# Moved turning products, two more split gate blocks, and a reordered router in a two-stage transformer kernel

## The reference, cut to what matters

```
proj = rmsnorm(x, g_mix) @ w_in          # q, k, v, index q/k, conv input, memory q, 3 x 1024 gate logits
o_a = top-k attention(rope(rmsnorm(q)), rope(rmsnorm(k)), v)      # 8 heads of 64, 2 key heads
o_b = silu(layernorm(causal depthwise conv(a * sigmoid(g), 31 taps)))
k_m, v_m = split(rmsnorm(mem, g_mem) @ w_mem_kv)                  # 256 memory tokens
o_m = memory attention(rmsnorm(q_m, g_qm), rmsnorm(k_m, g_km), v_m)
gates = sigmoid(gate_logits + b_gate)
x = x + (gates[0]*(o_a @ w_br_a) + gates[1]*(o_b @ w_br_b) + gates[2]*(o_m @ w_br_m)) @ w_o
h = rmsnorm(x, g_ffn)
router: best of 4 groups, then the 2 best of its 8 experts; out = sum of combine * (silu(a)*b) @ w_down
x = x + out
second block: silu(c) @ w_ada gives shifts, scales and gates of each layer (c has 1024 values)
```

## Time and profile before

| | us |
|---|---|
| median of 3 runs | 1892.06 |
| lowest and highest | 1891.32, 1894.72 |
| the profiled execution | 1889.99 |
| its span, first to last instruction | 1888.2 |
| TensorE busy | 1841.8 (98%) |
| VectorE busy | 1173.6 (62%) |
| ScalarE busy | 780.9 (41%) |
| mean DMA rate | 207 GB/s |

### The profile page before, as it was taken

The page is one execution under the profiler, slowest core; times in us unless marked ns, Lnnn a source line. Parts: engine busy times, 40 slices in busy tenths (PEclk is TensorE's granted clock), DMA queues, the critical chain, the costliest instruction groups (busy, mean ns, idle before and its releaser), DMA issues.

```text
span 1888.2 us, 29939 instructions
## 1 busy us (share of the span) xinstructions
PE 1841.8 (98%) x12476; PEld 1661.0 (88%) x12476; DVE 1173.6 (62%) x1777; ACT 780.9 (41%) x1081; POOL 0.2 (0%) x4
## 2 busy tenths in 40 slices
PE   9999999899999999999999999999999999989999
PEld 8879889788866668999988889999999997879999
DVE  3875456566666656877547458776876547545543
ACT  2325442534444445434443234344443444324432
POOL 0000000000000000000000000000000000000000
PEclk9999999899999999999999999999999999999999
DMA  8334311566899986876530057876686341043451
GB/s 316 132 130 158 137 68 35 239 233 241 321 395 370 376 320 236 342 302 260 199 134 23 23 204 287 331 301 258 256 320 253 157 157 45 6 152 133 181 201 68
DMA packets 65222, 391.59 MB, mean 207 GB/s; under 512 B 7360, under 2 KB 7488, under 8 KB 27328
## 3 DMA queue, kind: packets, MB, share of 16 engines
q1 hardware_dynamic: 64800, 389.61, 53.4%
q10 hardware_dynamic: 288, 0.08, 0.0%
HBM read 388.61 MB, written 1.05 MB: 206 GB/s over the span
## 4 chain that ended last, share of the span: by engine, by line
PE 88%; DVE 7%; ACT 2%; issue 1%; DMA 1%; DVEq 0%; SPq 0%; ACTq 0%
PE bank L510 87%; DVE region L2219 1%; PE bank L551 1%; ACT w_hi L1452 1%; DMA slab<-in_w_ffn_in 1%; DVE slab_low L1900 0%; DVE region L2182 0%; DMA slab<-in_w_up 0%; DVE region L1913 0%; DVE tiny L2181 0%; DVE region L2505 0%; DVE region L2482 0%; DVE region L2503 0%; DVE region L2173 0%; DVE region L2501 0%
## 5 line engine op out<-in xcount | busy, mean ns | idle before, releaser
L1900 DVE TENSOR_TENSOR slab_low<-slab,w_hi 128x2048 fp32r<-128x2048 f32 x152 | 348.2, 2292 | 201.8 <-ACT w_hi L1452 201.5
L510 PE MATMUL bank<-h_hi,w_hi 128*128 128x256 f32 x1408 | 391.6, 281 | 0.0
L510 PE MATMUL bank<-h_hi,slab_low 128*128 128x256 f32 x1408 | 390.9, 281 | 0.0
L510 PE MATMUL bank<-h_lo,w_hi 128*128 128x256 f32 x1408 | 380.2, 281 | 0.0
L1452 ACT ACTIVATE w_hi<-slab 128x2048 fp32r<-128x2048 f32 x152 | 291.0, 1916 | 151.1 <-DMA slab<-in_w_ffn_in 72.9
L510 PEld LDWEIGHTS bank<-h_hi,slab_low 128*128 128x128 f32 x1408 | 269.5, 191 | 0.0
L510 PEld LDWEIGHTS bank<-h_hi,w_hi 128*128 128x128 f32 x1408 | 264.7, 188 | 0.4
L510 PEld LDWEIGHTS bank<-h_lo,w_hi 128*128 128x128 f32 x1408 | 257.6, 188 | 0.0
L510 PE MATMUL bank<-gT_hi,d_hi 128*128 128x256 f32 x832 | 234.0, 281 | 0.8 <-DVE gT_lo L2097 0.8
L510 PE MATMUL bank<-gT_lo,d_hi 128*128 128x256 f32 x832 | 233.7, 281 | 0.0
L510 PE MATMUL bank<-gT_hi,d_low 128*128 128x256 f32 x832 | 233.6, 281 | 0.0
(11 more groups left out here) (279 smaller groups left out, 2826.0 us busy)
## 6 DMA issues: line engine op xcount, KB each, us to landing
slab<-in_w_ffn_in SPq DMA_DIRECT2D x88, 1024.0 KB, 8.6
slab<-in_w_up SPq DMA_DIRECT2D x64, 1024.0 KB, 8.8
region<-in_w_ada SPq DMA_DIRECT2D x112, 512.0 KB, 6.6
region<-in_w_ffn_out SPq DMA_DIRECT2D x44, 1024.0 KB, 4.8
region<-in_w_down SPq DMA_DIRECT2D x32, 1024.0 KB, 5.5
slab<-in_w_in SPq DMA_DIRECT2D x23, 1024.0 KB, 4.8
slab<-in_w_mix_in SPq DMA_DIRECT2D x20, 1024.0 KB, 7.9
hT<-in_w_ada SPq DMA_DIRECT2D x32, 512.0 KB, 5.7
```

The lines of the kernel that those rows point to most:

```text
L510: return nc.tensor.matmul(o, lhsT, rhs, start=start, stop=True, skip_group_check=True)
L1900: V_.tensor_tensor(slab_low[slot][:, :], slab[slot][:, :], w_hi[h % 3][:, :].bitcast(F), ALU.subtract)\
```

## The change

The three turning products are made behind all four blocks of memory queries, and the two duplicating products behind all four key blocks; ScalarE copies the duplicated key behind the four key copies accordingly. GATES_PLAIN is 2, so 22 gate blocks are split, there are 11 split slabs, and the convolution's sums are taken ahead of gate blocks 4 and 8. VectorE makes in_lo and the first slab's low part ahead of the four scalings of qm and km, the second slab's behind them. In the router ScalarE copies htok_lo directly behind htok_hi and signals tok_ready there, and makes the permutation copies ahead of the first weight slab's high part. Three warming products are left of the five ahead of the first unit. SyncE issues c behind the slabs of the second unit instead of ahead of all.

```diff
--- before.py
+++ after.py
@@ -162,7 +162,7 @@
 SHORT_FIRST, OUT_EARLY = 2, 4
 FFN_UNITS = 11
 GATHER_PLACES = 3
-GATES_PLAIN = 4
+GATES_PLAIN = 2
 VALUES = P + 8
 FIRST = P + 8
 SCORES_AT = {2: (0, 1), 3: (2, 3), 4: (4, 5), 5: (6, 7)}
@@ -848,7 +848,7 @@
             def moe():
                 members = [u for u in UNITS if u.seg == 0]
                 slabs_of(members[0])
-                keep_warm(5)
+                keep_warm(3)
                 for s in range(2):
                     ring_free(s)
                 for kc in range(KD // 2):
@@ -983,21 +983,17 @@
                     pair_sum(sq[:, 1:3, :])
                     pair_sum(sq[:, 3:5, :])
                     pair_sum(sq[:, 5, :])
-                if b == 15:
-                    pe.wait_ge(S["qka_normed"], w("qka_normed"))
-                    for x in range(2):
-                        pair_sum(B1["qa"][:, 2 * x:2 * x + 2, :], "rot", "dve")
-                    pair_sum(B1["ka"], "rot", "dve")
                 conv(b) if b < 8 else queries(b - 8) if b < 12 else memory(b - 12)
+            pe.wait_ge(S["qka_normed"], w("qka_normed"))
+            for x in range(2):
+                pair_sum(B1["qa"][:, 2 * x:2 * x + 2, :], "rot", "dve")
+            pair_sum(B1["ka"], "rot", "dve")
             for i in range(KD):
                 pe.wait_ge(S["memh"], w("memh"))
-            keys = projection(B1["memh"], 4, "act")
-            for b in range(4):
-                if b == 2:
-                    pe.wait_ge(S["ka_roped"], w("ka_roped"))
-                    for x in range(2):
-                        pair_sum(B1["ka"], f"dup{x}")
-                keys(b)
+            project(B1["memh"], 4, "act")
+            pe.wait_ge(S["ka_roped"], w("ka_roped"))
+            for x in range(2):
+                pair_sum(B1["ka"], f"dup{x}")
             vslab = [arrive().rearrange("p (k c) -> p k c", k=KD) for _ in range(2)]
             for t in range(NT):
                 ps = product("act")
@@ -1629,10 +1625,9 @@
                         rsqrt_of(take()[:, 0:n], rsB[:, 0:n], 1.0 / 64, C("small", 0, 1), "rs")
                 evac(B1["qm"][:, c, :])
             for c in range(4):
-                if c == 2:
-                    for x in range(2):
-                        evac(B1["kdup"][:, x, :])
                 evac(B1["km"][:, c, :])
+            for x in range(2):
+                evac(B1["kdup"][:, x, :])
             act.wait_ge(S["read_by_act"], w.n["read_by_act"])
             nc.scalar.activation(sq[:, 0:4, :], B1["qm"], ACT.Square)
             nc.scalar.activation(sq[:, 4:8, :], B1["km"], ACT.Square).then_inc(S["qkm_sq"], 1)
@@ -1701,20 +1696,20 @@
             for t in range(NT):
                 for x in range(2):
                     evac(htok_hi[:, t, x * 512:(x + 1) * 512], 512)
+            for t in range(NT):
+                for x in range(2):
+                    evac(htok_lo[:, t, x * 512:(x + 1) * 512], 512)
+            act.wait_ge(S["read_by_act"], w.n["read_by_act"])
+            act.sem_inc(S["tok_ready"], 1)
             act.wait_ge(S["router_top2"], w("router_top2"))
             for t in range(NT):
                 m = nc.scalar.activation(route("e21", t, 1), route("e8", t, 8)[:, 1:2], ACT.Exp,
                                          bias=route("nv1", t, 1))
             m.then_inc(S["router_exp"], 1)
-            up_high(0)
-            for t in range(NT):
-                for x in range(2):
-                    evac(htok_lo[:, t, x * 512:(x + 1) * 512], 512)
-            act.wait_ge(S["read_by_act"], w.n["read_by_act"])
-            act.sem_inc(S["tok_ready"], 1)
-            up_high(1)
             evac(permT[:, 0:2, :].rearrange("p i t -> p (i t)"), 512)
             evac(permT[:, 2, :])
+            up_high(0)
+            up_high(1)
             moe()
 
             for l in range(LAYERS):
@@ -2220,16 +2215,16 @@
                                                      ALU.mult, ALU.add))
             later()
             dve.sem_inc(S["conv_y"], 1)
+            dve.wait_ge(S["in_high"], w("in_high"))
+            dve.wait_ge(S["memh_used"], w("memh_used"))
+            V_.tensor_tensor(in_lo[:, :, :], hT[:, :, :], in_hi[:, :, :].bitcast(F), ALU.subtract)\
+                .then_inc(S["in_split"], 1)
+            gate_low(0)
             for x in range(4):
                 nm = "qm" if x < 2 else "km"
                 scale_rs(B1[nm][:, 2 * (x % 2):2 * (x % 2) + 2, :], col("g_qm" if x < 2 else "g_km"), 2)
             dve.sem_inc(S["qkm_normed"], 1)
-            dve.wait_ge(S["in_high"], w("in_high"))
-            dve.wait_ge(S["memh_used"], w("memh_used"))
-            V_.tensor_tensor(in_lo[:, :, :], hT[:, :, :], in_hi[:, :, :].bitcast(F), ALU.subtract)\
-                .then_inc(S["in_split"], 1)
-            for k in range(2):
-                gate_low(k)
+            gate_low(1)
             ps = take()
             for c in range(4):
                 ins = V_.scalar_tensor_tensor(B1["y"][:, c, :], ps[:, 0:T], -1.0 / 512, B1["y"][:, c, :],
@@ -2617,6 +2612,8 @@
                     sp.dma_start(d_raw[b], source(unit, "down")).then_inc(S[f"d_in{b}"], 16)
                 for n, unit in enumerate(members):
                     up_load(unit, source(unit, "up"))
+                    if n == 1 and unit.seg == 0:
+                        sp.dma_start(c_act, a["c_2"][0:1, :].broadcast_to([P, D])).then_inc(S["c_in"], 16)
                     if n == 1 and gate_sem:
                         sp.wait_ge(S[gate_sem], w(gate_sem))
                     if n:
@@ -2685,7 +2682,6 @@
                 m = a[part + ("_in_2" if which == "up" else "_out_2")]
                 row = (unit.group * FFN_UNITS + unit.x) * P
                 return m[row:row + P, :]
-            sp.dma_start(c_act, a["c_2"][0:1, :].broadcast_to([P, D])).then_inc(S["c_in"], 16)
             stream([u for u in UNITS if u.seg < 2], source)
 
             for l in range(LAYERS):
```

## The result

The change took the kernel from 1892.72 us (median of 4 runs, 1891.32 to 1894.72) to 1879.78 us (median of 4, 1878.06 to 1884.34): ratio 0.9935, 95% interval 0.9914 to 0.9955, a gain of 12.9 us (by the interval 8.5 to 16.3). The forecast was 1881.1. The profiled run of the changed kernel, 1884.34 us with a span of 1882.6, was the slowest of its four.

What follows compares the result with a forecast made beforehand. TensorE was taken as the bound, busy 1841.8 of 1888.2 us. The terms 3.45 + 1.06 + 6.45 = 10.96 us, off the median 1892.06, gave 1881.1; forecast 1880 to 1882.5 (0.60), whole range 1878.5 to 1885.5.

Steps and rivals of the forecast that it cites:

- Part 1: Turning products: a plain projection block fills the 3.88 us gap ending at 101.00, leaving 0.43 idle; 3.45 us saved.
- Parts 2 and 3: Gate blocks: two more split blocks save 1.06 us; the first split block, 10.3 us earlier, waits for nothing.
- The side remark on the old order: VectorE with scalings first: the first low part would come at 145.5 and stall TensorE by 3.4 us.
- Part 4: Router: the wait on htok_lo goes and the first expert unit starts 6.45 us earlier, 5.1 if the slab lands late.
- Clock rival: Router: narrow products, less warming and waiting lower the clock before the first unit; costs 2.2 us, 1883.3; chance 0.23.
- Give-back rival: Expert stage goes by its weights, so the router's gain returns as a wait; 4.5 us left, 1887.5; chance 0.06.
- Slower rival: Router: up to ten transfers share the engines and the first slab lands last; 8.6 us slower, 1900.7; chance 0.03.
- Late low parts: First split gate blocks wait for a late low part; costs up to 4.5 us, 1885.6; chance 0.05.
- the allowance for the spread of the runs: Range's low end: 1880 less 1.7, half the 3.4 us spread of three runs, rounded to 1878.5.
- the 2.1: Whole kernel: before's median of 1892.06 us was 2.1 above its profiled run; the same difference was taken for the changed kernel.

Runs made afterwards that it cites:

- turn_only: Kernel before with only the three turning products moved behind the last memory block and the duplicating ones behind the keys; 1887.61 us.
- gap_filled: Kernel before with eight warming products added ahead of the wait for the turning products, no work saved; 1890.41 us.
- router_only: Kernel before with the router's changes alone (htok_lo copied at once, permutation copies earlier, three warming products, c later); 1891.17 us, repeated unaltered 1889.57 us.
- after_again: The changed kernel measured again, unaltered; 1880.06 us.
- y_first: Changed kernel with the copies of y on ScalarE and VectorE put ahead of the slab splits in the expert steps; 1879.82 us.
- scalings_first: Changed kernel, 22 split blocks included, with VectorE's four scalings back ahead of in_lo and the low parts; 1889.61 us.
- router_turn_padded: Changed kernel with 20 split blocks and VectorE's old order, plus sixteen tiny TensorE instructions at the kernel's start; 1882.02 us.
- router_and_turn: Changed kernel without the two additional split blocks and with VectorE's old order; 1885.55 us.
- c_first: Changed kernel with c issued ahead of the first slab's transfers, as before; 1883.36 us.
- turn_and_22: Kernel before with the moved turning and duplicating products, 22 split gate blocks and VectorE's new order, router as before; 1885.45 us.

## Why the prediction was right, step by step

**Part 1, 3.45 us.** Right: 0.43 us idle left as worked out, 3.4 us at the first unit (turn_only). What the step lacked is the clock: I took the 1.00 of the earlier trace rows behind the gap as this kernel's behaviour, and it was one execution's. Two other profiles have 0.50 there, at a cost of 2.6 and 1.5 us. The medians (4.5 in turn_only, 1.8 from gap_filled without any work saved) suggest that the gap was worth another 1 to 2 us; that this is the clock's doing is not shown.

**Parts 2 and 3, 1.06 us and no wait.** Right. Up to the first split block after is 10.5 us shorter; the steps give 3.45 + 2 x 3.41 = 10.3. Behind the last gate block both profiles of after are 4.76 us ahead of before (108.27 against 113.03 behind the turning products), where the parts give 3.45 + 1.06 = 4.51, and 1.09 of it are the split blocks'. The first low part was 4.4 us early (I had 4.6). The second is done at 144.6 in a profile whose turning products start 1.1 us earlier than before's, as forecast with 145.6. The side remark on the old order failed: 5.76 us and not 3.4, because one subtraction of 2.29 was left out of its chain. The sum did not rest on it.

**Part 4, 6.45 us.** Right in mechanism, 0.5 too large. Without the router's part the first unit would stand 188.90 + 2 x 2.88 = 194.66 behind the first split block; it stood at 188.77 and 188.70, 5.9 to 6.0 gained. The slabs were issued 179.15 behind the first split block, where before's row with the two blocks gives 325.83 - 152.41 + 5.76 = 179.18: I had them 0.3 earlier, and landing after 4.8 us where it was 5.1 to 5.2. The waits (1.09 and 1.03 us, "about 1 us"), the full clock and c in time came as forecast.

**Clock rival (0.23).** It did not come in either profile of the changed kernel, but it is real, and the waits it went with can be read off. Nine profiles here have the early copy of htok_lo. With 1.0 to 1.4 us idle ahead of the first unit (after, after_again, y_first, scalings_first, router_turn_padded) none of five shows half clock at the first unit; with 2.3 to 2.9 (router_only, its repeat, router_and_turn, c_first) three of four do. I had priced it as a matter of warming products; what goes with it is how late the slab lands. The Trainium skill, "TensorE: Matmul & The Clock Gate", Part 1, has the low clock as the default; at the first unit the traces had it only behind waits of over 2 us, and there not every time.

**Give-back rival (0.06).** Not as I had it: the weight stream does not set the pace (372.29 against 371.85 us for the stage). But a part of the gain is given back at single places, 3.2 us in one profile of two, where a late slab holds up an unrelated copy. **Slower rival (0.03).** Did not come: tokens were ready early, ten transfers were under way at once, and the first slab landed sooner, not last. **Late low parts (0.05).** Would have come with the old order on VectorE, by 5.76 us, and at more than the 4.5 us it was priced at: 9.5 in the median (scalings_first).

**The size.** At the first unit the gain is 10.7 us in both profiles (0.25 more than the sum up to the gates, 0.5 less behind them), in the spans 5.6 and 10.5, in the medians 12.1 to 12.9. The median of 1879.78 is 0.2 under the forecast's own 1880 to 1882.5 and within the whole range only by the allowance for the spread of the runs. Leaving aside the first profile, which was the slowest run of its four, the difference is not in after: the profiled run of before lay 2.1 us below the median of the runs shown (2.7 below the later one), the second profiled run of after only 0.6 below its own. I carried the 2.1 over to after as if it were the chip's; much of it may have belonged to the gap, which the change removes.

## What to carry to other kernels

A gap of some us on a TensorE that is otherwise full costs its own length and, in some executions, a half-clocked stretch behind it: price it from several runs, and not from the clock of one profile. When two chains release the same instruction, value their edits together; here each was worth 1.9 us on top of the other and the pair 7.3 (turn_and_22, the undo of both and of the cut in warming products, with a slab that landed after 7.3 us). In an in-order engine, work whose input is ready belongs ahead of work that waits for a DMA.

## What was not expected of the hardware

The gap of 3.9 us ahead of the turning products, the same instructions in the same order, was followed by 1.00 in the profile of before and by 0.50 for 6.9 and 3.4 us in the two profiles of router_only. The time of the first 1 MB slab from issue to landing took 5.0 to 7.3 us, depending on what else was moved: with c ahead of it 6.2 to 7.3, with a code transfer in its flight and no c ahead 6.4 to 6.5, with neither 5.0 to 5.5. And executions of one program differ by the places of their half-clocked stretches: both profiles of after have one near 1093, 6.8 us long in the first and 3.4 in the second.
